# Modulation vectors between the gate/up chunks, the first attention beside the glu product, the context prepared during the second down product

## The reference

```
# block 1
h = x + 0.5 * swiglu(rmsnorm(x), ffn1_w_gate, ffn1_w_up, ffn1_w_down)        # 2048 -> 5504 -> 2048
q, k, v, u = split(rmsnorm(h) @ w_in)                                        # 1024 each
y_ssm = gelu(scan(u)); y_ssm = y_ssm * sigmoid(y_ssm @ w_glu + b_glu)
y_att = dilated_attention(q, k, v)                                           # 16 heads of 64
h = h + concat(rmsnorm(y_ssm), rmsnorm(y_att)) @ w_out
x1 = rmsnorm(h + 0.5 * swiglu(rmsnorm(h), ffn2_w_gate, ffn2_w_up, ffn2_w_down))
# block 2
shift, scale, gate       = split(silu(c) @ w_mod + b_mod, 3)                 # 2048 -> 6144, one vector
shift_c, scale_c, gate_c = split(silu(c_ctx) @ w_mod + b_mod, 3)
u   = layer_norm(x1) * (1 + scale) + shift
u_c = layer_norm(ctx) * (1 + scale_c) + shift_c
p, p_c = u @ w_in_2, u_c @ w_in_2[:, :N_KV]
out = branches(p, p_c) @ w_out_2                                             # mLSTM and attention
x_new = layer_norm(ALPHA * x1 + gate * out, ln_w, ln_b)
```

## Time and profile before

| | |
|---|---|
| median of 3 runs | 3583.09 us (3579.24 to 3588.93) |
| profiled execution | 3578.13 us, span of the core 3576.3 us |
| TensorE | 3403.4 us busy, 95% of the span, mean granted clock 0.975 |
| VectorE, ScalarE, GpSimd | 55%, 46%, 8% busy |
| DMA | 618.57 MB, mean 173 GB/s |

### The profile page before, as it was taken

How to read it: one execution, slowest core, us unless ns; L and a number is a source line. 1 busy time by engine, 2 the same in 40 slices (tenths; PEclk the granted TensorE clock), 3 DMA queues, 4 the chain that set the end, 5 groups by cost and what they waited for, 6 DMA issues and landing times.

```text
span 3576.3 us, 43679 instructions
## 1 busy us (share of the span) xinstructions
PE 3403.4 (95%) x15894; PEld 2774.7 (78%) x15894; DVE 1954.1 (55%) x2267; ACT 1645.8 (46%) x2005; POOL 303.0 (8%) x357
## 2 busy tenths in 40 slices
PE   8999999999988999999999799999999999999986
PEld 7888888886765878888888578777777777888775
DVE  5444455568677454455544554546554665445555
ACT  5444444443376344444433554444444545544333
POOL 0000036166600000000000000000000100000000
PEclk9999999999998999999999899999999999999998
DMA  7666655554467456666555746544435553566543
GB/s 226 188 188 188 191 189 189 186 180 142 131 207 237 153 170 189 188 188 189 186 186 189 244 145 185 155 132 156 142 112 157 158 159 101 154 194 204 171 148 124
DMA packets 318741, 618.57 MB, mean 173 GB/s; under 512 B 19256, under 2 KB 27728, under 8 KB 317696
## 3 DMA queue, kind: packets, MB, share of 16 engines
q1 hardware_dynamic: 316160, 606.25, 55.1%
q0 software_dynamic: 2432, 10.31, 0.8%
HBM read 614.39 MB, written 2.10 MB: 172 GB/s over the span
## 4 chain that ended last, share of the span: by engine, by line
PE 85%; DVE 6%; ACT 4%; DMA 3%; issue 2%; SPq 0%; ACTq 0%; DVEq 0%
PE acc L254 21%; PE acc L256 21%; PE acc L255 21%; DVE w_lo L222 3%; DMA w_raw<-in_w_mod 2%; PE pst L659 2%; PE pst L661 2%; PE acc L661 2%; PE acc L659 2%; PE acc L660 2%; PE pst L660 2%; ACT w_hi L216 2%; PE pst L2277 1%; PE pst L2259 1%; PE pst L1997 1%
## 5 line engine op out<-in xcount | busy, mean ns | idle before, releaser
L222 DVE TENSOR_TENSOR w_lo<-w_raw,w_hi 128x1024 fp32r<-128x1024 f32 x1160 | 1454.6, 1260 | 1356.7 <-ACT w_hi L216 1353.8
L216 ACT ACTIVATE w_hi<-w_raw 128x1024 fp32r<-128x1024 f32 x1160 | 1222.9, 1059 | 1532.1 <-PE acc L256 1135.0
L254 PE MATMUL acc<-w_hi,act_hi 128*128 128x512 f32 (+1 forms) x3552 | 1410.8, 397 | 30.0 <-DVE w_lo L222 26.4
L255 PE MATMUL acc<-w_lo,act_hi 128*128 128x512 f32 (+1 forms) x3552 | 1387.2, 391 | 0.0
L256 PE MATMUL acc<-w_hi,act_lo 128*128 128x512 f32 (+1 forms) x3552 | 1386.7, 390 | 0.0
L254 PEld LDWEIGHTS acc<-w_hi,act_hi 128*128 128x128 f32 x3552 | 674.9, 190 | 175.0 <-DVE w_lo L222 21.0
L256 PEld LDWEIGHTS acc<-w_hi,act_lo 128*128 128x128 f32 x3552 | 673.7, 190 | 138.4
L255 PEld LDWEIGHTS acc<-w_lo,act_hi 128*128 128x128 f32 x3552 | 675.0, 190 | 131.3 <-issue 0.5
L659 PE MATMUL pst<-w_hi,g_hi 128*128 128x512 f32 x344 | 136.5, 397 | 0.0
L659 PE MATMUL acc<-w_hi,g_hi 128*128 128x512 f32 x344 | 136.3, 396 | 0.0
L660 PE MATMUL pst<-w_lo,g_hi 128*128 128x512 f32 x344 | 136.1, 396 | 0.0
(11 more groups left out here) (430 smaller groups left out, 2285.5 us busy)
## 6 DMA issues: line engine op xcount, KB each, us to landing
w_raw<-in_w_in SPq DMA_DIRECT2D x400, 512.0 KB, 3.7
w_raw<-in_ffn_w_down SPq DMA_DIRECT2D x168, 512.0 KB, 3.6
w_raw<-in_ffn_w_gate SPq DMA_DIRECT2D x160, 512.0 KB, 3.7
w_raw<-in_ffn_w_up SPq DMA_DIRECT2D x160, 512.0 KB, 3.7
w_raw<-in_w_mod SPq DMA_DIRECT2D x96, 512.0 KB, 4.7
w_raw<-in_w_out SPq DMA_DIRECT2D x64, 512.0 KB, 4.5
w_raw<-in_w_branch_a SPq DMA_DIRECT2D x32, 512.0 KB, 4.5
w_raw<-in_w_branch_b SPq DMA_DIRECT2D x32, 512.0 KB, 4.2
```

Of the source, the lines that this page charges most:

```text
L216: act.activation(w_hi[:, s % SLOTS, :], w_raw[:, s % SLOTS, :], ACT.Copy).then_inc(w_hi_done, 1)
L222: dve.tensor_tensor(w_lo[:, s % SLOTS, :], w_raw[:, s % SLOTS, :], w_hi[:, s % SLOTS, :].bitcast(F32), ALU.subtract).then_inc(w_lo_done, 1)
L254: pe.matmul(o, xh, wh, start=k == 0, stop=False)
L255: pe.matmul(o, xh, wl, start=False, stop=False)
```

## The change

- **w_mod leaves the stream.** The jobs mod and mod_gate are gone. The 12 blocks of w_mod are taken up by loop passes of the two gate/up products: blocks 0 to 8 in ffn1's blocks 1 to 9, blocks 9 to 11 in ffn2's blocks 1 to 3. GpSimd loads the chunks into a ring of two buffers. TensorE multiplies them as they are, unsplit, in f32: the stationary operand is 32 columns (c and c_ctx of tile k, and 30 that are not used), the moving one 256 columns, and the four products of a chunk go to four column groups (PSUM partitions 0, 32, 64, 96) of one bank. A mod chunk follows the stream chunks 0, 2, 4, 6, 8, 10, 12 and 13 of a pass. After a block ScalarE copies 128x256, TensorE sums and turns it with `pick` (2 small products), VectorE adds b_mod.
- **The first attention** runs beside glu, two steps behind each of its 8 chunks, the last four behind the sigmoid. glu uses only `acc[:, 0]`, so its second half waits until the first is fetched.
- **w_out**: only two tiles of att are turned ahead; the others follow chunk by chunk, and the order of the turns is `upto=(6, 8, 8, 12, 14, 16, 16, 16)`.
- **The context** is loaded in two halves by GpSimd, normed and turned (transposes of 4 tiles, scale and shift at the fetch) during the second down product; ctx_k starts without turns.
- **The scan's parameters**: the two C tables are loaded after ffn1's mod blocks, and their loops run in 16 groups in place of 8.
- **The end**: statistics by bn_stats in `wo_fetch`, then two fused passes over quarters, each with its output DMA.

```diff
-JOBS = [("ffn1", None, None), ("w_u", 8, 2), ("w_qkv", 8, 6), ("glu", 4, 2), ("mod", 8, 8), ("w_out", 8, 4), ("ffn2", None, None),
-        ("mod_gate", 8, 4), ("ctx_k", 8, 2), ("ctx_v", 8, 4), ("ctx_kv", 8, 2),
+JOBS = [("ffn1", None, None), ("w_u", 8, 2), ("w_qkv", 8, 6), ("glu", 4, 2), ("w_out", 8, 4), ("ffn2", None, None),
+        ("ctx_k", 8, 2), ("ctx_v", 8, 4), ("ctx_kv", 8, 2),
...
+        MOD_BLOCKS = {"ffn1": (1, NB - 1, -1), "ffn2": (1, 4, 8)}
+        MOD_BEHIND = (0, 2, 4, 6, 8, 10, 12, 13)
...
+        def mod_loads_pool(pool, name):
+            first_mod, end_mod, shift = MOD_BLOCKS[name]
+            for n in range(8 * (first_mod + shift), 8 * (end_mod + shift)):
+                if n >= 2:
+                    pool.wait_ge(mod_used, n - 1)
+                pool.dma_start(mod_ring[int(name == "ffn2")][n % 2][:].rearrange("p (k n) -> p k n", k=2),
+                               cols(A["w_mod_2"], 2 * (n % 8), n // 8 * BLK)).then_inc(mod_ready[n % 2], 16)
+        def mod_chunk_pe(pe, n_use, blk, n):
+            pe.wait_ge(mod_ready[n % 2], blk * 64 + 16 * (n // 2 + 1))
+            if n == 0:
+                pe.wait_ge(mod_copied, blk + 1)
+            for kk in range(2):
+                k = 2 * n + kk
+                c = c_pairs[:, k:k + 16, :].rearrange("p k v -> p (k v)")
+                for hc in range(2):
+                    j, at_ = 32 * (2 * kk + hc), (2 * kk + hc) * SEQ
+                    mm = pe.matmul(pst[j:j + 32, 2, 0:SEQ], c, mod_ring[n_use][n % 2][:, at_:at_ + SEQ],
+                                   start=n == 0, stop=n == 7)
+            mm.then_inc(mod_used, 1)
+        def mod_pick_pe(pe, blk):
+            pe.wait_ge(mod_copied, blk + 2)
+            pe.wait_ge(mod_added, blk + 1)
+            o = pst[:, 3, 0:8].rearrange("p (hc c v) -> p c hc v", hc=2, c=2)
+            for c in range(2):
+                mm = pe.matmul(o[:, c], mod_nat[:, c * P:(c + 1) * P], pick[:], start=True, stop=True)
+            mm.then_inc(mod_picked, 1)
...
+                block_product(pe, s + 8, c + 8, act_hi, act_lo, 1, 8, p, between, n=width(b))
+                if blk is not None:
+                    mod_pick_pe(pe, blk)
+                elif first(b) and n_use == 0:
+                    pe.wait_ge(c_silu, 2)
...
             pool.tensor_scalar(pr(RED), pr(T1), 3.1415925, -3.1415925, ALU.min, ALU.max).then_inc(sp_ready, 1)
+            mod_loads_pool(pool, "ffn1")
+            pool.wait_ge(mod_used, 72)
...
+        def glu_pe(pe):
+            for m in range(2):
+                if m:
+                    pe.wait_ge(fetched[0], p0 + 2)
+                for j in range(4):
...
+                    mm.then_inc(w_used, 1)
+                    between()
+            for s in range(GLU_CHUNKS * ATT1_PER_CHUNK, ATT1_STEPS):
+                attention1_step_pe(pe, s)
...
+        CX_STATS = ((0, 16), (1, 22))
+        CX_TURN_AT = ((), (4, 6, 8, 10), (2, 4, 6, 8), ())
...
+            for n, (h, cs) in enumerate(END_PARTS):
+                o = resid[:, h, cs]
+                steps.did(dve.scalar_tensor_tensor(out=o, in0=o, scalar=row_mv[:, h, 0:1], in1=ln_w_row[:, cs],
+                                                   op0=S_, op1=M_))
+                if n == 0:
+                    dve.wait_ge(cn_root, 6)
+                    steps.did(dve.reciprocal(rstd, norm_root))
+                steps.settle()
+                dve.scalar_tensor_tensor(out=o, in0=o, scalar=rstd[:, h:h + 1], in1=ln_b_row[:, cs],
+                                         op0=M_, op1=A_).then_inc(end_done, 1)
```

More of the change, by code:

```diff
@@ L307, in norm_dve, with turn_act @@
             norm_diag_dve(dve, name)
-        def turn_act(act, name, gain=None, dst=0, bias=None):
+        def turn_act(act, name, gain=None, dst=0, bias=None, tiles=None):
             t0, _, n, _ = turns[name]
-            for k in range(n):
+            for k in tiles or range(n):
                 act.wait_ge(nt_turned, t0 + k + 1)
@@ L320, in turn_act, with turn_dve @@
                 ins.then_inc(nt_hi, 1)
[L322 removed]
+        def turn_dve(dve, name, gain=None, dst=0, bias=None, tmp=None, tiles=None):
             t0, _, n, _ = turns[name]
[L324 removed]
+            for k in tiles or range(n):
                 dve.wait_ge(nt_hi, t0 + k + 1)
@@ L1549, in mod_turn_pe @@
-        def mod_turn_pe(pe, after, use):
-            for m in range(2):
-                pe.wait_ge(fetched[m], AT[after][1] + 1)
-            src = (mod_nat, mod_nat_gate)[use]
-            for t in range(MOD_TILES[use]):
-                mm = pe.matmul(pst[:, 0, 2 * t:2 * t + 2], src[:, t * P:(t + 1) * P], pick[:], start=True, stop=True)
-            mm.then_inc(mod_turned, 1)
-        def wo1_step_pe(pe, s):
-            if s == 0:
-                mod_turn_pe(pe, "w_out", 0)
-        def wo1_step_dve(dve, s):
-            if s == 1:
-                mod_col_dve(dve, 0)
@@ L2457, in _ @@
             norm_act(act, "att", att, junk_lo_half)
-            turn_act(act, "att", gains[:, 2, 8:16], dst=8)
-            stream_split(act, "w_out")
+            turn_act(act, "att", gains[:, 2, 8:16], dst=8, tiles=(0, 1))
+            stream_split(act, "w_out", after=att_turns(turn_act), unrolled=True)
             for p in range(LEAD):
@@ L2581, in _ @@
             y_turn_pe(pe)
-            stream_pe(pe, "glu", turning=StateOutputs(pe))
-            for par in range(2):
-                pe.wait_ge(y_stored[par], 2)
-            mod_pe(pe, "mod", 0, spread(attention1_step_pe, pe, ATT1_STEPS, "mod"))
-            stream_pe(pe, "w_out", spread(wo1_step_pe, pe, 2, "w_out", skip=8), TurnedFirst(pe, ("ssm", ssm_y), ("att", att)))
-            pe.wait_ge(mod_done, 1)
+            glu_pe(pe)
+            for m in range(2):
+                pe.wait_ge(fetched[m], AT["w_out"][1] + 1)
+            stream_pe(pe, "w_out", turning=TurnedFirst(pe, ("ssm", ssm_y), ("att", att),
+                                                       upto=(6, 8, 8, 12, 14, 16, 16, 16)))
             for m in range(2):
```

446 lines of the change are left out of this document (248 added, 198 removed).

## The result

The changed kernel takes **3482.06 us** (median of 4 runs, 3481.26 to 3482.43), the kernel before 3583.07 (3579.24 to 3588.93): a ratio of 0.9722, 95% interval 0.971 to 0.9733. Forecast were 3497, in 3478 to 3550 (3480 to 3512 without the rivals, of which the measured time is near the low end). The span of the profiled execution went from 3576.3 to 3479.5 us, by 96.8 where the sum had 82.5.

A forecast was written before the change was run, and what follows sets the result against it. TensorE, busy 95% of the span, bounds the kernel, while job mod is paced by transfers and splitting. Terms sum to -82.5 us from 3576.3; forecast 3497 us (chance 0.62), own range 3480 to 3512, 3478 to 3550 with C, D and A's cheap end.

The forecast's parts named there:

- Part 5: Mod chunks in the ffn loops: 0.86 us of TensorE each, 96 chunks, +83 us; ends 0.76 and 2.05 us a chunk.
- Rival A: Mod chunks: column groups overlap only in pairs, 1.40 us a chunk, 52 us more, 3549 us; chance 0.11.
- Rival B: Mod chunks: column groups do not overlap at all, 2.05 us a chunk, 114 us more, 3611 us; chance 0.06.
- Part 6: Rest of the modulation: two small products a block against pick, 0.62 us a block, 12 blocks; +8 us.
- Part 8: Start of the w_mod ring: TensorE stalls of 1.4 and 9.7 us, +11 us once; 3 us more for the tightest load.
- Rival C: Ring or DMA rings late: two waits of 2 us a block add some 40 us, 3537 us; chance 0.11.
- Part 1: glu, attention and norm: 148 us from glu's first matmul to w_out's first turn become 68, -80 us; bounds 60 to 85.
- Rival D: Attention beside glu is bound by handoffs between engines: 20 to 25 us more, 3520 us; chance 0.10.
- Part 2: w_out: the 64 small modulation products and the stall before att's first turn go, -18 us; bounds 12 to 20.
- Part 3: ffn2's end to ctx_k's end: 131.3 us become 46, as ctx_k starts at the last fetch; -85 us, bounds 80 to 87.
- Part 4: Kernel end: 27.4 us from the last fetch to the span's end become 18.9, -8.5 us; bounds -6 to -10.
- Part 7: Context: 32 transposes in eight groups during ffn2's down product, +4 us with the waits.

## Why the prediction was right, step by step

The forecast held for the reasons given, with errors of both signs, and it is in part luck that they nearly cancel.

- **Part 5, the term that decides**: 0.86 us a chunk was forecast, 0.77 is seen at a chunk, and 0.80 by the loop passes (51.33 us, where 51.6 were forecast, against 44.94 without the products); the 96 cost 75 (by the gate product, 2033.0 against 1958.0 with the loads alone) to 77 us, not 83. The switch was right (0.33 against 0.34). The term that was mis-sized is the factor 1.24, carried over from the 32-column products: with 256 columns four products take 0.43 us, as long as one. The lower bound, 0.76, was the truth; why the short products cost more than that, no run here shows.
- **Rival A**, the rule of strict order from the Trainium skill (TensorE: Matmul & The Clock Gate, The mechanism) carried over to the two instructions of an f32 product, gave 1.40 us a chunk. The trace has 0.77, and in two groups 1.19, and four instructions start together where that reading has them one pair after the other: the trace disagrees with that reading. **Rival B** needed 2.05: that is the price in one group, 2.04, so the sum behind it was sound and only its condition false.
- **Part 6**: 0.62 us a block was forecast; from 122.18 over the four instructions to the second stream matmul 0.45 are measured, 12 blocks 5.5 us.
- **Part 8**: waits of 1.4 and 9.7 us were forecast, 1.6 and 8.65 seen; forgotten was the clock behind the long one, 1.6 us. The 3 us for a tight ring were nothing. **Rival C**, two late waits a block, would by its own terms add 12 x 4 = 48 us, not 40; none of them came.
- **Part 1**: 68 us forecast, 66.9 measured. The stall of 4 was 3.3, and 1.6 of clock. Rival D fell: between the chunks no step waits, and only the last heads do, in the tail.
- **Part 2**: -18 forecast, -24.6 measured. This is beyond its bounds of 12 to 20. The two stalls and the run of tiny products were each followed by a stretch at 1.2 GHz that cost 1.7 to 2.7 us, and no term had it, though the second of the earlier trace rows showed 0.93: some 4 us. Another 1.3 are the rest of the first stall, of which the sum had 3.5 of 4.78 us and all went.
- **Part 3**: 46 us forecast from the end of the last fetch to the gate product, 45.2 measured. ctx_k starts as that fetch ends and then waits for nothing but its stream:

```profile
1983.93 0.39 PE L813 MATMUL pst<-w_hi,g_lo 128*128 128x512 f32 x1
1987.92 0.80 PE L266 MATMUL acc<-w_hi,act_hi 128*128 128x512 f32 x1 [3.60 <-DVE resid L855]
```

- **Part 4**: 18.9 us forecast, 17.6 measured. (The terms as listed add up to 18.1.) The passes take 1.28 us each, not 1.22. Against that the root's table load, 1.28 us, comes at 3452.1, before the last fetch, the root itself (0.20) lies under the first pass, and the last output ends 3.1 us behind the last vector instruction, not 3.8.
- **Part 7**: 4 forecast, 3.4 measured.
- **Left out**: +7.1 us in the second block, some 5 of them longer busy time at a lower clock.

So the added costs were forecast too dear by some 11 us (parts 5 to 8, by the seams), the gains too small by 10 (parts 1 to 4), and 7 us were left out on the other side: near enough to the 14.3 by which the sum missed.

## What to carry over

Four f32 products with 32 stationary columns each took TensorE the time of one when they went to four column groups, and they could be put where TensorE is full, since the DMA had room. They are not free: 96 chunks cost some 76 us, of which the visits, 0.34 us each, are 33, so do several at a visit. Price a stall with the slow starts that may stand behind it, 1.6 us and more here, and do not take a busy TensorE for a fast one: it came out of 10 us of two-column products at half clock, and bare attention steps that followed a wait stayed at half clock for 24 us. Measure an edit at the next seam, since a program that is unchanged behind it can vary by 8 us.

## What the runs showed that was not expected

- Three of four f32 products of 256 columns in different column groups cost 0.02 us together: 0.75 us for one, 0.77 for four, 1.19 for four in two groups, 2.04 for four in one.
- Attention steps alone, behind a wait of 1.84 us, ran at a granted clock of 0.50 with TensorE busy for 24.37 of 24.40 us, 3.58 us a step in place of 1.94.
- The same second block took 1421.7 to 1430.2 us, with waits that differ by 3 us at most; the rest is the clock.
- DMA moved 280 GB/s beside the running stream without a wait.
